# Norm borders of a three-block transformer kernel: the last tile in token halves, high parts first, and one combined sum for the double norm

## The reference, cut to what matters

```
def rmsnorm(x, g):
    y = x * rsqrt(mean(x * x) + 1e-6)
    return y * g
def modulate(x, g, shift, scale):
    return rmsnorm(x, g) * (1 + scale) + shift
# per block
h = modulate(x, norm_mix_g, sh_m, sc_m);  x = x + g_m * (mixer(h) @ w_out)
h = modulate(x, norm_ffn_g, sh_f, sc_f);  x = x + g_f * ((act(a) * g) @ w_down)    # a, g = split(h @ w_in)
# after two blocks: x = rmsnorm(x, final_g); then the third block; at the end x = rmsnorm(x, g_final)
```

## Time and profile before

| | |
|---|---|
| median of 3 runs | 1987.98 us (1987.39 to 1991.22) |
| the profiled execution | 1991.48 us, of it 1989.7 us span |
| TensorE busy | 1923.1 us (97% of the span) |
| VectorE busy | 1034.7 us (52%) |
| ScalarE busy | 451.9 us (23%) |
| GpSimd busy | 1184.4 us (60%) |
| granted TensorE clock, mean | 0.985 of full speed |

### The profile page before, as it was taken

How to read it: one execution, slowest core, us unless ns; L and a number is a source line. 1 busy time by engine, 2 the same in 40 slices (tenths; PEclk the granted TensorE clock), 3 DMA queues, 4 the chain that set the end, 5 groups by cost and what they waited for, 6 DMA issues and landing times.

```text
span 1989.7 us, 25330 instructions
## 1 busy us (share of the span) xinstructions
PE 1923.1 (97%) x8824; PEld 1551.2 (78%) x8824; DVE 1034.7 (52%) x1529; ACT 451.9 (23%) x774; POOL 1184.4 (60%) x907
## 2 busy tenths in 40 slices
PE   5999999999999999999999999999988899999998
PEld 4787868888888887667788888887766688888886
DVE  7566256666655453466766663233877453323222
ACT  3302342211210022352221211112228421111100
POOL 3743326788887955324688787746540256666773
PEclk7999999999999999999999999999989999999999
DMA  7432223455554422111455553322210023222332
GB/s 305 177 117 75 96 95 106 170 190 192 204 193 174 172 96 85 53 52 55 157 191 193 197 189 117 105 96 85 74 59 17 27 82 104 95 95 95 106 105 74
DMA packets 67375, 242.23 MB, mean 122 GB/s; under 512 B 7498, under 2 KB 7882, under 8 KB 67314
## 3 DMA queue, kind: packets, MB, share of 16 engines
q1 hardware_dynamic: 65536, 237.01, 34.2%
q10 hardware_dynamic: 1778, 4.37, 0.6%
HBM read 239.25 MB, written 2.10 MB: 121 GB/s over the span
## 4 chain that ended last, share of the span: by engine, by line
PE 86%; DVE 7%; ACT 3%; issue 2%; DMA 2%; POOL 1%; DVEq 0%; SPq 0%; ACTq 0%; POOLq 0%
PE gemm L447 23%; PE gemm L448 23%; PE gemm L449 23%; DMA w_raw<-wstream 2%; DVE b_score L1630 1%; PE mix L650 1%; PE gemm L474 1%; PE gemm L476 1%; PE gemm L475 1%; DVE b_top L1625 1%; PE mix L447 1%; PE gemm L1046 1%; PE gemm L803 1%; DVE sq_acc L1365 1%; PE mix L449 1%
## 5 line engine op out<-in xcount | busy, mean ns | idle before, releaser
L431 POOL TENSOR_TENSOR w_lo<-w_raw,w_hi 128x1024 fp32r<-128x1024 f32 x302 | 734.9, 2433 | 25.2
L447 PE MATMUL gemm<-h_hi,w_hi 128*128 128x512 f32 x1616 | 634.0, 392 | 20.8 <-DVE h_lo L1186 14.6
L448 PE MATMUL gemm<-h_lo,w_hi 128*128 128x512 f32 x1616 | 630.1, 390 | 0.0
L449 PE MATMUL gemm<-h_hi,w_lo 128*128 128x512 f32 x1616 | 630.1, 390 | 0.0
L428 POOL TENSOR_TENSOR pool_gate<-pool_gate 128x1 f32<-128x1 f32 x298 | 118.3, 397 | 734.4 <-PE gemm L449 592.8
L447 PEld LDWEIGHTS gemm<-h_hi,w_hi 128*128 128x128 f32 x1616 | 304.2, 188 | 90.2 <-issue 21.8
L429 POOL TENSOR_SCALAR w_hi<-w_raw 128x1024 fp32r<-128x1024 f32 x302 | 344.1, 1139 | 17.5 <-DMA w_raw<-wstream 17.5
L449 PEld LDWEIGHTS gemm<-h_hi,w_lo 128*128 128x128 f32 x1616 | 304.0, 188 | 63.8
L448 PEld LDWEIGHTS gemm<-h_lo,w_hi 128*128 128x128 f32 x1616 | 304.1, 188 | 62.0
L1080 DVE CUSTOM_DVE_ANT_0 ada_raw<-ada_raw,c_act 128x1024 f32<-128x1024 f32 x128 | 216.5, 1707 | 110.1 <-DMA ada_raw<-adastream 110.1
L449 PE MATMUL gemm<-p_hi,w_lo 128*128 128x512 f32 x528 | 205.4, 389 | 0.0
(11 more groups left out here) (339 smaller groups left out, 1972.0 us busy)
## 6 DMA issues: line engine op xcount, KB each, us to landing
w_raw<-wstream SPq DMA_DIRECT2D x302, 512.0 KB, 3.5
ada_raw<-adastream SPq DMA_DIRECT2D x128, 512.0 KB, 4.3
a_early<-adastream SPq DMA_DIRECT2D x8, 1024.0 KB, 11.9
out<-x_res SPq DMA_DIRECT2D x8, 256.0 KB, 2.2
c_act<-c_in ACTq DMA_DIRECT2D x2, 512.0 KB, 7.2
x_res<-x_in SPq DMA_DIRECT2D x2, 512.0 KB, 6.3
x_res<-x_in ACTq DMA_DIRECT2D x2, 512.0 KB, 9.0
b_dist<-const_in ACTq DMA_DIRECT2D x1, 512.0 KB
```

Of the source, the lines that this page charges most:

```text
L431: pool.tensor_tensor(wlo[s][:], raw[:, u % RAW, :], whi[s][:].bitcast(F32), ALU.subtract).then_inc(w_split, 1)
L447: pe.matmul(out_ap, w_h, r_h, start=first, stop=False)
L448: pe.matmul(out_ap, w_h, r_l, start=False, stop=False)
L449: return pe.matmul(out_ap, w_l, r_h, start=False, stop=last)
```

## The change

- **Halves.** The last residual tile is added in two halves of 256 tokens (`last_residual`), squared in two halves, and summed in two steps of two matmuls. The reciprocal is spread for the first 256 tokens into a bank of its own (`M[0]`), then for all four blocks into `rstdps`; tile 0 is scaled and rounded in halves too. The other seven tiles are whole, as before.
- **High parts first.** `first_tiles` waits for the high part only, does its two passes for all output tiles, and does the pass with the low part one tile of x later. This holds for all its fills.
- **One sum for the double norm.** The gain is replaced by the root of gain squared plus eps, and the bias of the root by eps squared; then a single sum gives the inverse of both norms together. The plain sum of x squared, which the normalised x still needs, is finished behind the spreading, and its root and reciprocal come after the fill.
- **Fewer unread matmuls.** `WARM` goes from (2, 4, 4, 14) to (1, 1, 2, 14): per ordinary border 1, 1 and 2 such matmuls where 2, 1 and 4 stood. Border 4 has 1 and 1 where 2, 3 and 4 stood.
- **Addresses.** `cols` is padded from 440 to 448 columns. The tiles behind it up to `pool_gate` (among them `c_act`, `cst`, `sq_tile`, `sq_acc`) lay 32 bytes past a multiple of 64 and now lie on one; `work`, `h_hi`, `h_lo`, `p_hi` and all behind them lay on multiples of 64 already and move up by 64 bytes. `w_raw`, `w_hi`, `w_lo` and `x_res` stay where they are.
- The loop over the squares on ScalarE is written out.

```diff
-WARM = (2, 4, 4, 14)
+WARM = (1, 1, 2, 14)
...
-        cols = sb("cols", [P, NCOL])
+        cols = sb("cols", [P, -(-NCOL // 16) * 16])
...
+        eps_sq = sb("eps_sq", [P, 1])
...
+                def low(k):
+
+                    pe.wait_ge(h_ready, KT * fill + k + 1)
+                    for u in range(count):
+                        s = (N0[phase] + u) % SPL
+                        mm = pe.matmul(G[u][:], whi[s][:, k * P:(k + 1) * P], Hlo[:, k, :], start=False, stop=(k == KT - 1))
+                        if k == KT - 1:
+                            mm.then_inc(pe_done, 1)
+
                 for u in range(count):
                     pe.wait_ge(gfree[u], G0[phase][u])
                 for k in range(KT):
                     if k in before:
                         before[k]()
-                    pe.wait_ge(h_ready, KT * fill + k + 1)
+                    w = slice(k * P, (k + 1) * P)
+                    pe.wait_ge(hhi_ready, KT * fill + k + 1)
                     for u in range(count):
                         if k == 0 and u % 2 == 0:
                             pe.wait_ge(w_split, N0[phase] + u + 2)
                         s = (N0[phase] + u) % SPL
-                        mm = three(G[u][:], whi[s][:, k * P:(k + 1) * P], wlo[s][:, k * P:(k + 1) * P],
-                                   Hhi[:, k, :], Hlo[:, k, :], k == 0, k == KT - 1)
-                        if k == KT - 1:
-                            mm.then_inc(pe_done, 1)
+                        pe.matmul(G[u][:], whi[s][:, w], Hhi[:, k, :], start=(k == 0), stop=False)
+                        pe.matmul(G[u][:], wlo[s][:, w], Hhi[:, k, :], start=False, stop=False)
+                    if k:
+                        low(k - 1)
+                low(KT - 1)
...
             def norm_scale(r):
+                borders[0] += 1
                 pe.wait_ge(sq_added, KT * r + KT - 1)
                 partial_sums(0, sqacc, True, False)
-                keep_warm(WARM[0])
-                pe.wait_ge(sq_ready, KT * (r + 1))
-                mm = partial_sums(0, sqt[:, 1, :], False, True)
+                c0, last = 0, sqt[:, 1, :]
                 if r == 4:
                     pe.wait_ge(gsq_added, KT)
-                    partial_sums(4, work[:, 2, :], False, False)
+                    c0, last = 8, work[:, 1, :]
+                    partial_sums(c0, work[:, 2, :], False, False)
+                keep_warm(WARM[0])
+                pe.wait_ge(sq_half, borders[0])
+                partial_sums(c0, last, False, True, (0, 1))
+                if r == 4:
                     pe.wait_ge(gsq_ready, KT)
-                    mm = partial_sums(4, work[:, 1, :], False, True)
-                mm.then_inc(norm_sum, 1)
-                keep_warm(3 if r == 4 else 1)
-
-            def token_rows(ps, c0):
-
-                for j in range(NTB):
+                else:
+                    pe.wait_ge(sq_ready, KT * (r + 1))
+                partial_sums(c0, last, False, True, (2, 3)).then_inc(norm_sum, 1)
+                keep_warm(WARM[1])
+
+            def token_rows(ps, c0, blocks=range(NTB)):
...
             def norm(r):
                 norm_scale(r)
+                c0 = 8 if r == 4 else 0
                 bc[0] += 1
-                bcast(rstdps, bc[0])
-                if r not in (0, 6):
-                    keep_warm(WARM[2])
+                pe.wait_ge(rstd_ready, bc[0])
+                token_rows(M[0], c0, (0, 1)).then_inc(bc_half, 1)
+                token_rows(rstdps, c0, (2, 3, 0, 1)).then_inc(rstd_bc, 1)
+                if r == 4:
+                    pe.wait_ge(sq_ready, KT * (r + 1))
+                    partial_sums(0, sqt[:, 1, :], False, True).then_inc(norm_sum, 1)
+                elif r != 6:
...
+            def last_residual(n, m, bank, gate):
+
+                dve.wait_ge(pe_done, n + 1)
+                for half, done in ((slice(0, HALF), last_half), (slice(HALF, T), gfree[bank])):
+                    dve.scalar_tensor_tensor(out=X[:, m, half], in0=G[bank][:, half], scalar=modv[:, gate + m:gate + m + 1],
+                                             in1=X[:, m, half], op0=ALU.mult, op1=ALU.add).then_inc(done, 1)
...
+            def border_inverses(c0):
+
+                borders[0] += 1
+                rms_n[0] += 1
+                dve.wait_ge(rms_ready, rms_n[0])
+                ready(dve.reciprocal(rst[:, c0:c0 + 4], rms[:, c0:c0 + 4]))
+                dve.wait_ge(bc_half, borders[0])
...
-                if first_gain is None:
-                    ready(inverse_rms(4, rms_n[0]))
-                else:
-                    ready(inverse_rms(4, rms_n[0]))
-                    dve.wait_ge(rstd_ready, inverses_done[0])
-
-                    rms_n[0] += 1
+                if first_gain is not None:
                     link(dve.tensor_tensor(a, a, first_gain, ALU.mult))
-                    link(dve.tensor_tensor(rst[:, 4:8], rst[:, 0:4], rst[:, 0:4], ALU.mult))
-                    dve.tensor_tensor(rst[:, 4:8], rst[:, 4:8], normps[:, 4:8], ALU.mult).then_inc(sig("second_mean"), 1)
-                    dve.wait_ge(rms_ready, rms_n[0])
-                    link(dve.reciprocal(rst[:, 8:12], rms[:, 8:12]))
-                    ready(dve.tensor_tensor(rst[:, 8:12], rst[:, 8:12], rst[:, 0:4], ALU.mult))
-                spread()
-
-                def scaled(k):
-                    dve.scalar_tensor_tensor(out=work[:, k % 4, :], in0=X[:, k, :], scalar=a[:, k:k + 1], in1=rstdps[:],
-                                             op0=ALU.mult, op1=ALU.mult).then_inc(t_ready, 1)
+                border_inverses(0 if first_gain is None else 8)
+
+                def scaled(k, part=slice(0, T), done=t_ready, bank=rstdps):
+                    dve.scalar_tensor_tensor(out=work[:, k % 4, part], in0=X[:, k, part], scalar=a[:, k:k + 1], in1=bank[:, part],
+                                             op0=ALU.mult, op1=ALU.mult).then_inc(done, 1)
...
-                scaled(0)
+                scaled(0, slice(0, HALF), t_half, M[0])
+                spread()
+                scaled(0, slice(HALF, T))
                 scaled(1)
                 for k in range(KT):
                     low(k)
                     if k + 2 < KT:
                         scaled(k + 2)
+                if first_gain is not None:
+                    rms_n[0] += 1
+                    ready(inverse_rms(4, rms_n[0]))
...
-                for k in range(KT):
+                act.wait_ge(t_half, borders[0])
+                act.activation(Hhi[:, 0, 0:HALF], work[:, 0, 0:HALF], ACT.Identity, bias=modv[:, shift:shift + 1])
+                act.wait_ge(t_ready, scaled[0] + 1)
+                act.activation(Hhi[:, 0, HALF:T], work[:, 0, HALF:T], ACT.Identity, bias=modv[:, shift:shift + 1]).then_inc(hhi_ready, 1)
+                for k in range(1, KT):
...
+                if gain is not None:
+                    link(act.activation(gain, col("final_g", 0, 8), ACT.Square))
+                    link(act.activation(gain, gain, ACT.Sqrt, bias=col("eps")))
+                for m in range(KT - 1):
+
+                    act.wait_ge(gfree[m % 4], m // 4 + G0[phase][m % 4] + 1)
+                    act.wait_ge(sq_added, KT * r + m - 1)
+                    act.activation(sqt[:, m % 2, :], X[:, m, :], ACT.Square).then_inc(sq_ready, 1)
+                    if gain is not None:
+                        act.wait_ge(gsq_added, m + 1)
+                        act.activation(work[:, m % 2, :], X[:, m, :], ACT.Square, scale=gain[:, m:m + 1]).then_inc(gsq_ready, 1)
+                m = KT - 1
+                borders[0] += 1
+                act.wait_ge(sq_added, KT * r + m - 1)
+                if gain is not None:
+                    act.wait_ge(gsq_added, m + 1)
+                for half, there, count, done in ((slice(0, HALF), last_half, borders[0], sq_half),
+                                                 (slice(HALF, T), gfree[3], G0[phase][3] + 2, sq_ready if gain is None else gsq_ready)):
+                    act.wait_ge(there, count)
+                    if gain is None:
+                        act.activation(sqt[:, 1, half], X[:, m, half], ACT.Square).then_inc(done, 1)
+                    else:
+                        act.activation(work[:, 1, half], X[:, m, half], ACT.Square, scale=gain[:, m:m + 1]).then_inc(done, 1)
...
-            act.wait_ge(sig("second_mean"), 1)
-            act.activation(rms[:, 8:12], rst[:, 4:8], ACT.Sqrt, bias=col("eps"), scale=1.0 / D).then_inc(rms_ready, 1)
+            act.wait_ge(sig("eps_sq_set"), 1)
+            roots(8, eps_sq[:])
+            act.activation(sqt[:, 1, :], X[:, KT - 1, :], ACT.Square).then_inc(sq_ready, 1)
             high_tiles(96)
+            roots(0, col("eps"))
```

More of the change, by code:

```diff
@@ L526, in down, with keep_warm, partial_sums @@
                             c += 1
-            def keep_warm(n):
+            def keep_warm(n, bank=M[0]):
                 for _ in range(n):
```

(28 more changed lines are left out.)

55 lines of the change are left out of this document (20 added, 35 removed).

## The result

The changed kernel takes **1997.74 us** (median of 20 runs, 1991.55 to 2006.62) against 1989.90 us for the kernel before beside it (20 runs). The ratio is 1.0042, 95% interval 1.0033 to 1.0051: 0.4% slower, where 0.5% faster was forecast (1978.0, full range 1973.5 to 1984.5). The profiled execution of the changed kernel took 1996.65 us, of it 1994.9 us span, at a mean granted clock of 0.986 (0.985 before).

A forecast was written before the change was run, and what follows sets the result against it. TensorE, busy 97% of the span, bounds the kernel, leaving gains only at borders and the first fill: 4.8 + 2.6 + 0.25 + 2.4 = 10.05 us off the median 1987.98 gives 1978.0 us, full range 1973.5 to 1984.5.

The forecast's parts named there:

- At nothing: Parts put at no gain or cost: the written-out loop, two small instructions for the gain, and the 32 byte shift.
- the 32 byte shift: Moved small tiles: put at nothing, since one ScalarE operation took 495 ns and 500 ns at places 32 bytes apart.
- The new addresses cost: Rival, chance 0.03: `h` and `p` 64 bytes off slow 6432 matmuls, at 3 ns each 19 us: 1997.
- matmuls more than 0.23 us apart: In the middle of a stage: one of the signs that would show the forecast wrong.
- ordinary borders 1, 2, 5: Each saves 1.2 us: 0.43 from halves ahead of the root, 0.75 from high parts first behind it.
- border 3: Forecast as an ordinary border like 1, 2 and 5: 1.2 us saved.
- border 4: Double norm with one root: 2.6 us saved if the clock falls; rival, chance 0.15, that it holds: 5.1.
- first fill: The very first fill: high passes run earlier, GpSimd starts 2.4 us earlier, and 2.4 us are saved.
- last border: 0.43 us won before the root, part lost behind it as tile 0's second half starts later: 0.25 us saved.
- half instructions: Halves at the borders: 0.47 us for one on VectorE, 0.95 for two half sums, 0.50 for rounding on ScalarE.
- the part ahead of the root: Halves up to the root at all six borders: TensorE's last sum ends 0.43 us earlier, bounds 0 and 0.6.
- the clock falls at every border: Rival, chance 0.06: fewer unread matmuls drop the clock at ordinary borders too, costing 2.85 us or more each: 1994.

The follow-up runs named there:

- b_new_places: The kernel before with only its tiles moved to the changed kernel's addresses; 2005.81 us, ratio 1.0088 to before.
- b_all_64: The kernel before with 64 unused bytes ahead of `x_res`, so every tile moves, weights' tiles too; 1989.00 us, ratio 1.0006 to before.
- a_old_places: The changed kernel with every tile back at its address of before, no instruction moved; 1984.48 us, ratio 0.9977 to before.
- a_best: The changed kernel at old addresses, six unread matmuls behind the first fill's first round, 1, 2, 4 at borders; 1981.71 us, ratio 0.9961 to before.
- a_warm: The changed kernel at old addresses with 1, 2, 4 unread matmuls at a border instead of 1, 1, 2; 1983.58 us, ratio 0.9974 to before.
- b_plus_64: The kernel before with 64 unused bytes ahead of `work`, moving `work`, `h`, `p` and all behind; 2005.91 us, ratio 1.0085 to before.

## Why the prediction was wrong

**The step that failed** is the one under "At nothing": "the 32 byte shift". It compared one ScalarE operation at two places and let that stand for all readers, the products among them, and so the sum has no term for them. The tiles that matter were in another clause, 64 bytes up, and only in a rival: "The new addresses cost", at 3 ns a product, with a chance of 0.03. That rival is what happened: 2.2 ns, and 6.5 for the 480 swapped products that it did not count, where it turned the sign at 1.6. In place of nothing the runs show 17 us (b_new_places). The fault was in the chance, not in the mechanism, though its reading (`h` and `p` off their old places) was incomplete: b_all_64 has them there and loses nothing. That its 1997 stands so near the measured 1997.74 is in part luck: 3 ns were put for 2.2, and a saving of 10 us of which the medians show 4.4. 6432 reads multiply any effect, no row bore on the place, and an unknown with a turning point of 1.6 ns in 227 (0.7%) should not have had 0.03. The sign put down for it, matmuls more than 0.23 us apart, could not have shown it either: 228.9 ns is printed as 0.23.

Taken apart by ratios: the change at old addresses gives -0.23%, the changed kernel has +0.42%, so the addresses cost it 0.65%. In the kernel before they cost 0.88%; the intervals of the two figures overlap.

**The other terms**, read from a_old_places against before (one profile each):

| term | forecast us | measured us |
|---|---|---|
| ordinary borders 1, 2, 5 | 1.2 each | 1.44, 1.21, 1.32 |
| border 3 | 1.2 | 0.14 (clock fell), and 0.86 more wait ahead of it |
| border 4 | 2.6; 5.1 if the clock holds | 5.4 (it held); 4.2 in the changed kernel (it fell) |
| first fill | 2.4 | 2.3, then 2.7 lost to the clock |
| last border | 0.25 | 0.4 (0.6 ahead of the root, -0.2 behind; from the changed kernel) |

Where the clock held, the terms of borders 1, 2 and 5 were right to 0.25 us, and the half instructions cost what was put (0.88 for two, 0.48 for one, 0.51 for rounding). The halved squares were done earlier than put, and the part ahead of the root gave 0.59 for 0.43. At border 4 of the changed kernel the clock fell 4.0 us behind the first sum, as put, but for 3.4 us instead of 6.8. (The rise before was at 1330.87, not 1330.83; that changes nothing.)

Still the sum of 10.05 came to 4.4 us in the medians. The first fill's term took the wait behind it as free. Where the clock fell in that wait, the 2.3 became a loss of 0.4. Nor was the wait for `sq_acc` (0.86) thought of. And the clock falls at one to three ordinary borders of an execution (in six of seven profiles with the halves, in none of the three with the old border and 226.7 ns), at 1.0 us (border 1 of the changed kernel) to 3.3 (border 3 of a_best). The rival "the clock falls at every border" was thus right in kind, at one border or a few instead of all. More unread matmuls did not settle it: the profile of a_warm has no such fall, that of a_best has one.

One error is of method: the saving was read from one profiled execution. The profiled run of a_old_places took 1981.31, 3.2 under its median, that of before 1991.48, 2.6 over the 1988.83 beside it. Their difference is the 10 us forecast, and the medians' is not. That agreement is chance. Between the two profiles the six borders give 9.9, the wait for `sq_acc` and the first fill take 1.3 away, and the stage between borders 4 and 5, in which nothing was gained by the change, is 1.6 us shorter (276.79 against 278.43): the clock fell in both, for 6.8 us in one and 10.2 in the other. Border 4 kept its clock and gave 2.8 more than was put; border 3 and the first fill gave less. How the executions at the medians differ is not known: no trace of one was taken.

## What to carry to other kernels

When a tile is added or padded, work out for every hot matmul the distance modulo 128 bytes between its weights' tile and its moving tile, and keep it at 0; a multiple of 64 alone is not enough. Look for such a loss in the distance between starts, or in the count of records in a window, since durations and idle times do not show it. The cost at 32, 64 and 96 bytes is measured for one kernel and one kind of product (512 columns, fp32r). Where an edit makes TensorE wait longer at one place, look at the granted clock right behind it before the gain is counted.

## What the runs showed of the hardware that was not expected

- The pace of 512-column fp32r products with new weights each time, by the distance modulo 128 bytes between their two tiles: 226.7 ns at 0, whatever the absolute place (0, 32, 64), and 233.3 at 32 and at 96. At 64 it is 228.9 with the weight chunk as the weights and 233.3 with `h` as the weights. So the distance alone does not fix the pace.
- In b_plus_64 one whole stage, from border 1 to border 2, ran at 233.3 ns (1582 products from 345.18 to 714.31), at full clock and usual traffic; the streams right ahead of it and behind it have 228.9 again. Its profiled run took 2012.88, 7 us above its median. 1502 records in 350 us and, behind border 2, 394 in 90:

```profile
350.00:700.00 350.00, 350.00 (x1502) 1.00 0.50 181
710.00:800.00 90.00, 88.27 (x394) 1.00 0.25 88
```

What put it there is open. So is the mechanism behind the distance itself; no run here looks into it.
- VectorE's addition of two SBUF tiles beside GpSimd's split ends 0.55 us behind the split, whenever it began (2.57 us long before, 2.72 with a start 0.17 us earlier); alone it takes 0.69 us.
